# Two-layer decoder trunk on one core: expert stages in 64-slot units, two side by side in TensorE's output, with plain float32 products and 2-MB weight transfers

## The chip, the cores and the metric

One Trainium2 chip, one core. The metric is the device time of one execution in microseconds; the kernel before takes 2580.95 us in the median of three runs.

## The reference, cut to what matters

Two layers of a decoder over 1040 tokens (16 meta tokens and 1024), each a mixer followed by a channel mixer. The mixers (convolution and sparse attention; a gated recurrence) are not touched. The channel mixer is a routed mixture of 32 gated MLPs, and each token goes to 2 of them:

```python
def grouped_expert_ffn(xf, eid, w_gate, w_up, w_down):
    ...
    def run(args):
        xblk, e = args
        return (jax.nn.silu(xblk @ w_gate[e]) * (xblk @ w_up[e])) @ w_down[e]
    ...
def hierarchical_moe(h, wg, bg, we, be, w_gate, w_up, w_down):
    ...
    g_p, g_idx = lax.top_k(g_prob, 1)
    ...
    e_top, e_idx = lax.top_k(e_logits, TOP_K_INNER)
    gate = g_p * jax.nn.softmax(e_top, axis=-1)
    expert = (g_idx * EXPERTS_PER_GROUP + e_idx).reshape(-1)
    y_pairs = grouped_expert_ffn(xf, expert, w_gate, w_up, w_down).reshape(n_tok, TOP_K_INNER, d)
    y = jnp.einsum('nkd,nk->nd', y_pairs, gate.astype(y_pairs.dtype))
```

The width is 1024, the inner width of an expert 512, all in float32. An expert has three matrices of 2 MB (6.29 million bytes together). Layer 0 routes 2080 token-expert pairs, layer 1 (where only the 1024 tokens are kept) 2048.

## The kernel before, in words

The program is a list of stages; each stage writes out what every engine does, in order, with semaphores between them. The stage that changes is `experts` (L1878), called once for each layer. The layer-0 call runs from about 757 to 1424 us of the profiled span, the layer-1 call from about 1892 to 2544 us.

A stage first sorts the pairs by expert: `route` on VectorE turns counts into blocks of 128 slots, an expert having at least one block, and small matrix products (`slots`, L2401) put each pair's number into its slot. The result is a list in SBUF: the number of blocks, each block's expert, and whether it is another expert than the block before (`meta_i`). Engines read it into registers.

Then it works block by block, in a loop whose order is written out by hand:

- SyncE (`load`, `reload`, L1953 to L1972) fetches the expert's weights in six chunks of 1 MB (two each for gate, up and down) into `raw`, with a condition that skips a block of the same expert. A chunk may be overwritten once VectorE has split it (`lo_done`).
- GpSimd gathers 128 rows of h into `x` (L2006), and later adds 128 weighted rows of output to the sums in HBM with one accumulating scatter (`scatter`, L2010), waited for before `y` is free again. Slots that are not used carry an index out of bounds and move nothing.
- TensorE turns x (8 transposes, L2312) and hidden (4 transposes, L2323) and makes the products. Each float32 product is made from three float32r products (`mm3`, L90): high by high, high by low, low by high. Its order in a turn is gate for the next block (with the transposes of hidden in its middle), up for the next block, transposes of x for the one after, down for this block.
- ScalarE and VectorE split every weight chunk into a high and a low float32r part (L2066 and L2218), and x and hidden too; ScalarE makes silu (L2075) and takes y out of PSUM (L2084), VectorE multiplies silu by up (L2231).

```python
def mm3(pe, out, stat, mov, start, stop):
    pe.matmul(out, stat[0], mov[0], start=start, stop=False)
    pe.matmul(out, stat[0], mov[1], start=False, stop=False)
    return pe.matmul(out, stat[1], mov[0], start=False, stop=stop)
```

`stay_warm` (L97) makes plain float32 products of 256 columns that nothing reads, six or seven of them at a stage's start. Behind the layer-0 stage `combine` reads the sums back (L1875); in layer 1 the last two blocks stay on the chip and are added in `last_norm` (class `Rest`).

Of the kernel before, what the change touches and what calls it, by code (L numbers as in the profile page):

```python
# [43 lines left out]
MAXB = -(-(2 * T + NE * (P - 1)) // P)  # L44
# [23 lines left out]
C_ROW = C_IB + MAXB  # L68
# [1407 lines left out]
class Picks:  # L1476


    def __init__(self, c):
# [4 lines left out]
        self.is_l, self.is_h = (c.sb("pick_" + n, [P, 2, NB, P], BF16, side=RIGHT) for n in ("isl", "ish"))  # L1484
# [39 lines left out]
    def place(self, dve, link, const, work, ranks, B, first, read, nth, made):  # L1524
# [8 lines left out]
        link(dve.tensor_scalar(at_i[:, :, B], at_i[:, :, B], P - 1, None, ALU.bitwise_and))  # L1533
        link(dve.tensor_copy(self.at_p[:, :, B], at_i[:, :, B]))
        link(dve.tensor_tensor(self.over[:, :, B], at[:, :, B], self.at_p[:, :, B], ALU.subtract))
        for j in range(2):
            for b in range(B.start, B.stop):
                col = 2 * (first * NB + b) + j
                for dst, at_c in ((self.is_l, C_LOW), (self.is_h, C_PAIR)):
                    ins = dve.tensor_scalar(dst[:, j, b, :], const[:, C_I128:C_I128 + P], self.at_p[:, j, b:b + 1],  # L1540
                                            const[:, at_c + col:at_c + col + 1], ALU.is_equal, ALU.mult)
# [275 lines left out]
SUM_CHUNKS, GAIN_CHUNK = (2, 3, 4, 5, 0), 1  # L1817


class Rest:  # L1820


    def __init__(self, c, name, bank, sets):
        self.up = c.sb(name + "_wu", [P, 4, EXPERT_CHUNK], F32R)
        self.bank = bank
        self.acc = [bank[:, 0:2, :], bank[:, 4:6, :]][0:sets]

    def w_hi(self, i):
        return self.up[:, i - 2, :]

    def w_lo(self, i):
        return self.up[:, i, :]

    def y_hi(self, e):
        return self.up[:, 0, e * D:(e + 1) * D]

    def y_lo(self, e):
        return self.up[:, 2, e * D:(e + 1) * D]

    def place(self, e):  # L1840
        return self.up[:, 1 + 2 * e, 0:T]
# [10 lines left out]
class Sums:  # L1852
# [8 lines left out]
    def rows(self, n):  # L1861
        return self.raw[0:toks(self.blocks[n]), SUM_CHUNKS[n // 2], (n % 2) * D:(n % 2) * D + D]

    def gain(self, j):
        return self.raw[:, GAIN_CHUNK, j * D:(j + 1) * D]
# [12 lines left out]
def experts(nc, name, const, picks, h_d, sum_d, wg_d, wu_d, wd_d, first, raw, sums, rest=None):  # L1878


    CH, NCH = EXPERT_CHUNK, EXPERT_CHUNKS
    nb = NB - first
    B = slice(first, NB)
    n_tok = T if first == 0 else SEQ
    with Ctx(nc) as c:
        n_own = NCH if rest is None else NCH - 2
        own_hi, own_lo = c.sb(name + "whi", [P, n_own, CH], F32R), c.sb(name + "wlo", [P, n_own, CH], F32R)

        def chunk(i, own, kept):
            if rest is None:  # L1890
                return own[:, i, :]
            return kept(i) if i in (2, 3) else own[:, i if i < 2 else i - 2, :]

        w_hi = [chunk(i, own_hi, rest and rest.w_hi) for i in range(NCH)]
        w_lo = [chunk(i, own_lo, rest and rest.w_lo) for i in range(NCH)]
        x = c.sb(name + "x", [P, D])
        x_hi, x_lo = c.sb(name + "xh", [P, KC, P], F32R), c.sb(name + "xl", [P, KC, P], F32R)
        sg, hid = c.sb(name + "sg", [P, FE]), c.sb(name + "hid", [P, FE])
        h_hi, h_lo = c.sb(name + "hh", [P, FE // P, P], F32R), c.sb(name + "hl", [P, FE // P, P], F32R)
        y = c.sb(name + "y", [P, D])  # L1900
        ix, sx = c.sb(name + "ix", [P, 1], I32), c.sb(name + "sx", [P, 1], I32)
# [8 lines left out]
        cnt_i = c.sb(name + "_ci", [P, NE], I32)  # L1910
        start_of, at_r, at_b = (c.sb(name + n, [P, 2, NB]) for n in ("_so", "_ar", "_ab"))
        at_i = c.sb(name + "_ai", [P, 2, NB], I32)
        in_b, is_pf = c.sb(name + "_inb", [P, 2, NB, MAXB], BF16), c.sb(name + "_ispf", [P, 2, NB, P])
        wide_done = c.sem(name + "_wide")
        gates, is_g, by_slot = t3("_gates", 2), c.sb(name + "_isg", [P, 2, NB, MAXB]), c.sb(name + "_bys", [P, MAXB])
        pair_i, tok_i = c.sb(name + "_pair", [P, MAXB], I32), c.sb(name + "_tok", [P, MAXB], I32)
        of_blk, row = c.sb(name + "_ofb", [P, 1]), c.sb(name + "_row", [1, 2 * MAXB + 1])
        meta_i = c.sb(name + "_meta", [1, 2 * MAXB + 1], I32)
        N_AT, E_AT, R_AT = 0, 1, 1 + MAXB
# [5 lines left out]
        hi_done = [c.sem(name + f"_hi{i}") for i in range(NCH)]  # L1925
        lo_done = [c.sem(name + f"_lo{i}") for i in range(NCH)]
        chain, act_sem, count_mm, rank_mm, rank_read, placed, hot_b, slots_mm, blk_done, blk_mm, listed, indexed, hot_g, by_slot_mm, by_slot_done = (
            c.sem(name + n) for n in ("_c", "_a", "_cm", "_m", "_rr", "_pld", "_hb", "_sm", "_bd", "_bm", "_ls", "_in", "_hg", "_bym", "_byd"))
        primed, x_half, x_half_hi = (c.sem(name + n) for n in ("_primed", "_xhf", "_xhh"))
        x_zero, ix_done, sx_done, ix_taken, sx_taken, x_in, x_tr, x_hi_done, x_lo_done, g_mm, u_mm, sg_done, hid_done, h_tr, h_hi_done, h_lo_done = (  # L1930
            c.sem(name + n) for n in ("_xz", "_ix", "_sx", "_ixt", "_sxt", "_x_in", "_x_tr", "_x_hi", "_x_lo", "_g_mm", "_u_mm", "_sg", "_hid",
                                      "_h_tr", "_h_hi", "_h_lo"))
        y_mm, y_taken, y_stored, y_free = (c.sem(name + n) for n in ("_y_mm", "_y_taken", "_y_stored", "_y_free"))
# [4 lines left out]
        FIRST_LOADS = (0, 1, 2)  # L1938

        block = c.block()  # L1940

        def bc(t, w):
            return t[:, B, :].broadcast_to([P, nb, w])
# [4 lines left out]
        def blocks_but_two(eng):  # L1948
            eng.wait_ge(listed, 1)
            return eng.snap(eng.value_load(meta_i[0:1, N_AT:N_AT + 1], min_val=NE - 2, max_val=MAXB - 2))  # L1950
# [1198 lines left out]
```

## Time and profile before

| | |
|---|---|
| runs, us | 2576.66, 2580.95, 2582.27 (median 2580.95) |
| profiled execution: its span, us (the page gives no other time of it) | 2577.0 |
| TensorE matmuls busy | 2426.1 us, 94% |
| VectorE busy | 2025.5 us, 79% |
| ScalarE busy | 1683.3 us, 65% |
| GpSimd busy | 653.5 us, 25% |
| bytes moved by DMA | 565.81 MB, mean 220 GB/s |
| expert stage of layer 0 | 757.2 to 1424.1 us |
| expert stage of layer 1 | 1891.5 to 2544.0 us |

Busy time is the union of an engine's instructions. Matmul records overlap, since each has its pipeline's length in it, so the pace of TensorE is read from one start to the next. A DMA share of 1 means that the core's 16 DMA engines had packets all the time.

### The profile page before, as it was taken

How to read it: one execution, taken by the hardware profiler on the slowest of the kernel's cores; microseconds unless marked ns; L12 is line 12 of the kernel's file. 1: busy time of each engine (PE TensorE's matmuls, PEld its weight loads, DVE VectorE, ACT ScalarE, POOL GpSimd, SP SyncE). 2: the span in 40 equal slices, each digit the busy share in tenths (PEclk: the TensorE clock that was granted, in tenths of full speed). 3: DMA queues.
4: the chain of work that ended last, by engine and by line, in shares of the span. 5: the costliest groups of instructions: out<-in, count | busy, mean ns of one | idle time of the engine just before them, and what ended most of it. 6: DMA issues, size and time to landing. Idle time of an engine off the chain costs nothing. (4 is left out here: it accounts for less than half of the span.)

```text
span 2577.0 us, 37706 instructions
## 1 busy us (share of the span) xinstructions
PE 2426.1 (94%) x12715; PEld 2077.8 (81%) x12715; DVE 2025.5 (79%) x2589; ACT 1683.3 (65%) x1814; POOL 653.5 (25%) x480
## 2 busy tenths in 40 slices
PE   9989998987979999999999599999979999999997
PEld 8979978885867888888888499997867888888885
DVE  4788876777889989999898544547779998998887
ACT  3369836666227788887887466663147888877775
POOL 0105814343002222222221412121013222223232
PEclk9999999997989999999999699999989999999999
DMA  5502354324349699988998411114259699999995
GB/s 181 134 13 87 83 99 128 105 67 136 101 148 405 228 346 375 366 322 316 320 376 290 173 58 36 39 34 159 94 204 356 234 353 369 376 370 363 376 373 191
DMA packets 121902, 565.81 MB, mean 220 GB/s; under 512 B 24119, under 2 KB 32567, under 8 KB 72528
## 3 DMA queue, kind: packets, MB, share of 16 engines
q1 hardware_dynamic: 96688, 513.25, 55.1%
q0 software_dynamic: 25120, 51.36, 7.2%
q8 instruction: 54, 0.88, 0.1%
q14 instruction: 40, 0.33, 0.0%
HBM read 575.32 MB, written 73.28 MB: 252 GB/s over the span
## 5 line engine op out<-in xcount | busy, mean ns | idle before, releaser
L2218 DVE TENSOR_TENSOR e0wlo<-e0raw,e0whi 128x2048 fp32r<-128x2048 f32 x214 | 487.1, 2290 | 59.8 <-ACT e0whi L2066 59.8
L2066 ACT ACTIVATE e0whi<-e0raw 128x2048 fp32r<-128x2048 f32 x214 | 409.9, 1915 | 90.3 <-PE e0banks L94 78.2
L2218 DVE TENSOR_TENSOR e1wlo<-e1raw,e1whi 128x2048 fp32r<-128x2048 f32 x138 | 313.2, 2286 | 43.4 <-ACT e1whi L2066 43.2
L2066 ACT ACTIVATE e1whi<-e1raw 128x2048 fp32r<-128x2048 f32 x138 | 263.9, 1913 | 40.0 <-PE e1banks L94 33.5
L92 PE MATMUL e0banks<-e0whi,e0xh 128*128 128x512 f32 x576 | 231.1, 401 | 2.9 <-DVE e0xl L2223 2.7
L94 PE MATMUL e0banks<-e0whi,e0xl 128*128 128x512 f32 x576 | 226.1, 392 | 0.0
L93 PE MATMUL e0banks<-e0wlo,e0xh 128*128 128x512 f32 x576 | 225.6, 392 | 0.0
L2218 DVE TENSOR_TENSOR e_wu<-e1raw,e_wu 128x2048 fp32r<-128x2048 f32 x70 | 160.2, 2290 | 17.8 <-ACT e_wu L2066 17.7
L92 PE MATMUL odd_banks<-h2T_hi,odd_w_hi 128*128 128x348 f32 x480 | 171.6, 357 | 0.8 <-DVE h2T_lo L2539 0.5
L2066 ACT ACTIVATE e_wu<-e1raw 128x2048 fp32r<-128x2048 f32 x70 | 134.2, 1918 | 50.4 <-PE e1banks L94 30.7
L93 PE MATMUL odd_banks<-h2T_lo,odd_w_hi 128*128 128x348 f32 x480 | 155.1, 323 | 0.0
L94 PE MATMUL odd_banks<-h2T_hi,odd_w_lo 128*128 128x348 f32 x480 | 155.1, 323 | 0.0
L92 PEld LDWEIGHTS e0banks<-e0whi,e0xh 128*128 128x128 f32 x576 | 108.6, 189 | 32.7 <-issue 11.3
L94 PEld LDWEIGHTS e0banks<-e0whi,e0xl 128*128 128x128 f32 x576 | 108.5, 188 | 23.2
L93 PEld LDWEIGHTS e0banks<-e0wlo,e0xh 128*128 128x128 f32 x576 | 108.8, 189 | 20.9
L92 PE MATMUL e1banks<-e1whi,e1xh 128*128 128x512 f32 x280 | 115.6, 413 | 6.4 <-DVE e1xl L2223 6.4
L2472 DVE TENSOR_TENSOR odd_w_lo<-odd_w_raw,odd_w_hi 128x1024 fp32r<-128x1024 f32 x18 | 22.3, 1239 | 119.4 <-ACT odd_w_hi L2468 119.4
L92 PE MATMUL e0banks<-e0whi,e0hh 128*128 128x512 f32 x280 | 112.1, 400 | 0.0
L94 PE MATMUL e1banks<-e1whi,e1xl 128*128 128x512 f32 x280 | 110.6, 395 | 0.0
L93 PE MATMUL e1banks<-e1wlo,e1xh 128*128 128x512 f32 x280 | 110.3, 394 | 0.0
L92 PE MATMUL e1banks<-e_wu,e1xh 128*128 128x512 f32 x280 | 109.1, 390 | 0.2 <-DVE e_wu L2218 0.2
L94 PE MATMUL e1banks<-e_wu,e1xl 128*128 128x512 f32 x280 | 109.2, 390 | 0.0
(526 smaller groups left out, 6898.2 us busy)
## 6 DMA issues: line engine op xcount, KB each, us to landing
e0raw<-in_moe_w_gate SPq DMA_DIRECT2D x72, 1024.0 KB
e0raw<-in_moe_w_up SPq DMA_DIRECT2D x72, 1024.0 KB
e0raw<-in_moe_w_down SPq DMA_DIRECT2D x72, 1024.0 KB
e1raw<-in_moe_w_gate SPq DMA_DIRECT2D x70, 1024.0 KB
e1raw<-in_moe_w_up SPq DMA_DIRECT2D x70, 1024.0 KB
e1raw<-in_moe_w_down SPq DMA_DIRECT2D x70, 1024.0 KB
qki_w_raw<-in_w_even SPq DMA_DIRECT2D x22, 512.0 KB, 5.8
pre<-in_conv_band SPq DMA_DIRECT2D x32, 320.0 KB, 3.0
```

What stands on the lines that cost most here:

```text
L92: pe.matmul(out, stat[0], mov[0], start=start, stop=False)
L93: pe.matmul(out, stat[0], mov[1], start=False, stop=False)
L94: return pe.matmul(out, stat[1], mov[0], start=False, stop=stop)
L2066: act.activation(w_hi[i], raw[:, i, :], ACT.Copy).then_inc(hi_done[i], 1)
L2218: dve.tensor_tensor(w_lo[i], raw[:, i, :], w_hi[i].bitcast(F32), ALU.subtract).then_inc(lo_done[i], 1)
L2472: eng.tensor_tensor(self.w_lo[:, n % 2, :], self.raw[:, n % 2, :], self.w_hi[:, n % 2, :].bitcast(F32), ALU.subtract).then_inc(self.lo_don ...
```

## The change

- Slots are counted in units of 64 (`UNIT`), and the units of a layer are laid in two halves: column g has unit g in partitions 0 to 63 and unit g + half in 64 to 127. The list now has an entry for each unit, and the number of columns.
- The products are plain float32: no high and low parts, no splits on ScalarE and VectorE. Each product of 128 stationary columns becomes two of 64, `both`: one per half, with that half's own expert's weights, into partitions 0 to 63 and 64 to 127 of the same bank.
- Six whole matrices are held (three for each half), raw only, each fetched as one 2-MB transfer once the products of the one before it have been made (`used`). A transfer is skipped where the half's expert stays.
- x and hidden are copied from PSUM once; ScalarE takes the first half of x, VectorE the second.
- The scatter is made in two parts, one per half, each waited for before the next.

```diff
-MAXB = -(-(2 * T + NE * (P - 1)) // P)
+UNIT = P // 2
+MAXU = (2 * T + NE * (UNIT - 1)) // UNIT
+MAXC = -(-MAXU // 2)
...
-            def reload(chunks, g):
-                e = sp.value_load(meta_i[0:1, bass.ds(g + E_AT, 1)], min_val=0, max_val=NE - 1)
-                new = sp.value_load(meta_i[0:1, bass.ds(g + R_AT, 1)], min_val=0, max_val=1)
-                for i in chunks:
-                    sp.wait_ge(lo_done[i], g)
-                    load(i, e, new)
+            def load(w, s, e, new=None, into=None):
+                into = 3 * s + (w if into is None else into)
+                src = (wg_d, wu_d, wd_d)[w][bass.ds(e, 1), :, :].rearrange("a (p c) n -> (a p) c n", p=P)
+                dst = whole[into].rearrange("p (c n) -> p c n", c=(8, 8, 4)[w])
...
+            def reload(matrices, g):
+                e = [expert_of(u) for u in (g, g + half)]
+                new = [sp.value_load(meta_i[0:1, bass.ds(u + R_AT, 1)], min_val=0, max_val=1) for u in (g, g + half)]
+                for w in matrices:
+                    sp.wait_ge(used[2 * w + 1], g)
+                    for s in range(2):
+                        load(w, s, e[s], new[s])
+            for w in range(3):
+                load(w, 0, 0)
+            m = columns_but_two(sp)
+            half = sp.snap(sp.value_load(meta_i[0:1, H_AT:H_AT + 1], min_val=NE // 2, max_val=MAXC))
+            e = expert_of(half)
+            for w in range(3):
+                load(w, 1, e)
+            reload((0, 1), 1)
+            reload((0, 1), 2)
+            reload((2,), 1)
...
-                pool.indirect_dma_start(sum_d, bass.IndirectOffsetOnAxis(sx[:, 0:1].bitcast(U32), 0), y[:], None,
-                                        bounds_check=n_tok - 1, oob_is_err=False, compute_op=ALU.add).then_inc(y_stored, 16)
-                pool.wait_ge(y_stored, g * 16 + 16)
-                pool.sem_inc(y_free, 1)
+                for s in range(2):
+                    pool.indirect_dma_start(sum_d, bass.IndirectOffsetOnAxis(sx[:, s:s + 1].bitcast(U32), 0), rows[:], None,
+                                            bounds_check=n_tok - 1, oob_is_err=False, compute_op=ALU.add).then_inc(y_stored[s], 16)
+                    pool.wait_ge(y_stored[s], stored)
+                    pool.sem_inc((y_half, y_free)[s], 1)
...
             def turn(g):
-                split_h(g)
-                for i in WG:
-                    split_w(i, g + 2)
+                take_h(g)
                 silu(g + 1)
-                for i in WU:
-                    split_w(i, g + 2)
-                split_x(g + 2)
-                split_w(4, g + 1)
+                take_x(g + 2)
                 take_y(g)
-                split_w(5, g + 1)
...
-                link(dve.tensor_scalar(cnt_i[:], xt_ps[:, 1, 0:NE], float(P - 1), None, ALU.add))
-                link(dve.tensor_scalar(cnt_i[:], cnt_i[:], 7, None, ALU.arith_shift_right))
+                link(dve.tensor_scalar(cnt_i[:], xt_ps[:, 1, 0:NE], float(UNIT - 1), None, ALU.add))
+                link(dve.tensor_scalar(cnt_i[:], cnt_i[:], 6, None, ALU.arith_shift_right))
                 link(dve.tensor_scalar(nblk[:], cnt_i[:], 1.0, None, ALU.max))
                 link(dve.tensor_tensor_scan(pend[:], one32[:], nblk[:], 0.0, ALU.mult, ALU.add))
+                link(dve.tensor_scalar(half_i[:], pend[:, NE - 1:NE], 1.0, None, ALU.add))
+                link(dve.tensor_scalar(half_i[:], half_i[:], 1, None, ALU.arith_shift_right))
+                link(dve.tensor_scalar(half_f[:], half_i[:], float(UNIT), None, ALU.mult))
...
+            def both(out, stat, chunk, a, start, stop):
+
+                for s in range(2):
+                    last = pe.matmul(out[HALF[s], :], stat[:, HALF[s]], raw[NCH * s + chunk][:, a], start=start, stop=stop)
+                return last
...
                 for k in range(4 * (i % 2), 4 * (i % 2) + 4):
-                    a = slice((k % 4) * FE, (k % 4 + 1) * FE)
-                    last = mm3(pe, ps[:], (x_hi[:, k, :], x_lo[:, k, :]), (w_hi[i][:, a], w_lo[i][:, a]),
-                               k == 0, k == KC - 1)
+                    last = both(ps, xt[:, k, :], i, slice((k % 4) * FE, (k % 4 + 1) * FE), k == 0, k == KC - 1)
                 last.then_inc(used[i], 1)
```

How the order of instructions moves. First TensorE, in the loop of the layer-0 stage, from the end of up to the start of down (`e0x` is x, `xh`/`xl` and `hh`/`hl` the parts of turned x and hidden, `xt` and `ht` the same turned and whole, `e0raw` and `e0own` homes of raw weights). Before:

```order
L92 MATMUL e0banks<-e0whi,e0xh 128x512
L93 MATMUL e0banks<-e0wlo,e0xh 128x512
L94 MATMUL e0banks<-e0whi,e0xl 128x512
L2308 ISA
L2312 MATMUL e0banks<-const,e0x 128x128 x8
L92 MATMUL e0banks<-e0whi,e0hh 128x512
L93 MATMUL e0banks<-e0wlo,e0hh 128x512
L94 MATMUL e0banks<-e0whi,e0hl 128x512
```

and now, from the loop's start:

```order
L2224 MATMUL e0banks<-e0own,e0xt 64x512 x8
L2249 MATMUL e0banks<-const,e0hid 128x128 x4
L2224 MATMUL e0banks<-e0own,e0xt 64x512 x8
L2224 MATMUL e0banks<-e0raw,e0xt 64x512 x16
L2233 ISA
L2238 MATMUL e0banks<-const,e0x 128x128 x8
L2230 ISA
L2224 MATMUL e0banks<-e0raw,e0ht 64x512
L2224 MATMUL e0banks<-e0own,e0ht 64x512
```

The order of gate, transposes, up and down stays. What was three products of 128x512 is two of 64x512, and the full-width transposes stand between the half-width products twice in a turn.

Second GpSimd, the same loop, from the gather on. Before:

```order
L2037 COPY e0ix<-e_tok 128x1
L2038 REGISTER_ALU
L2006 DMA e0x<-h,e0ix 128x1024
L2012 ISA
L2012 COPY e0sx<-e_tok 128x1
L2015 DMA sum<-e0y,e0sx 1040x1024
L2017 ISA
```

and now:

```order
L2024 COPY e0ix<-e_tok 128x1
L2025 REGISTER_ALU
L1992 DMA e0x<-h,e0ix 128x1024
L1998 ISA
L1998 COPY e0sx<-e_tokh 128x2
L2002 DMA sum<-e0y,e0sx 1040x1024
L2004 ISA
L2002 DMA sum<-e0y,e0sx 1040x1024
```

The second scatter, behind the first one's wait, stands ahead of the next gather. Third SyncE, the loads of the loop, now:

```order
L1947 DMA e0own<-in_moe_w_gate 128x4096
L1947 ISA
L1947 DMA e0own<-in_moe_w_gate 128x4096
L1947 DMA e0raw<-in_moe_w_up 128x4096 x2
L1950 ISA
L1950 TENSOR_LOAD e_meta
```

There were six of 128x2048 to a turn; there are six of 128x4096, with eight reads of the list instead of four.

## Rows read from the trace of the kernel before

**Rows 1.** The page: its span and part 1, engines' busy time.
```profile
span 2577.0 us, 37706 instructions
...
PE 2426.1 (94%) x12715; PEld 2077.8 (81%) x12715; DVE 2025.5 (79%) x2589; ACT 1683.3 (65%) x1814; POOL 653.5 (25%) x480
```

**Rows 2.** Windows (first line: columns): the expert stages of both layers.
```profile
core 0: us, PE busy (x) PEld busy (x) DVE busy (x) ACT busy (x) POOL busy (x), PEclk, DMA share, GB/s
757.20:1424.10 666.90, 656.93 (x3118) 541.24 (x3118) 594.13 (x373) 522.28 (x366) 152.86 (x143) 0.99 0.89 330
1891.50:2544.00 652.50, 638.48 (x3026) 525.68 (x3027) 582.74 (x371) 506.82 (x357) 168.00 (x136) 0.99 0.93 343
```

**Rows 3.** Timeline (start and length in us, engine, line, operation): TensorE in layer 0.
```profile
999.62 0.39 PE L93 MATMUL e0banks<-e0wlo,e0xh 128*128 128x512 f32 x1
...
999.85 0.19 PEld L92 LDWEIGHTS e0banks<-e0whi,e0xh 128*128 128x128 f32 x1
...
1001.21 0.39 PE L94 MATMUL e0banks<-e0whi,e0xl 128*128 128x512 f32 x1
```

**Rows 4.** SyncE: timeline from 856 us, its waits in layer 0.
```profile
856.41 2.51 SPq L1963 DMA_DIRECT2D e0raw<-in_moe_w_gate  x2
...
892.41 0.34 SPq L1963 DMA_DIRECT2D e0raw<-in_moe_w_gate  x1
...
SPq L1963 <- DVE e0wlo L2218: 392.7, 193, 4.7
```

**Rows 5.** The page, part 6: gate weights, two transfers to a block.
```profile
e0raw<-in_moe_w_gate SPq DMA_DIRECT2D x72, 1024.0 KB
...
e1raw<-in_moe_w_gate SPq DMA_DIRECT2D x70, 1024.0 KB
```

**Rows 6.** Windows: four stretches of layer 0's stage.
```profile
757.00:770.00 13.00, 6.16 (x53) 5.00 (x54) 11.36 (x47) 6.49 (x6) 3.18 (x4) 0.50 0.80 295
...
790.00:820.00 30.00, 27.51 (x121) 22.48 (x122) 28.80 (x18) 23.16 (x16) 11.21 (x4) 0.94 1.02 419
840.00:900.00 60.00, 60.00 (x287) 49.65 (x286) 54.48 (x32) 48.05 (x34) 13.90 (x14) 1.00 0.63 217
940.00:1100.00 160.00, 160.00 (x755) 132.01 (x754) 145.42 (x81) 128.80 (x91) 37.33 (x36) 1.00 0.99 371
```

**Rows 7.** Groups by line: layer 0's weight splits.
```profile
L2218 DVE TENSOR_TENSOR e0wlo<-e0raw,e0whi 128x2048 fp32r<-128x2048 f32 x214 | 487.1, 2290 | 59.8 <-ACT e0whi L2066 59.8
L2066 ACT ACTIVATE e0whi<-e0raw 128x2048 fp32r<-128x2048 f32 x214 | 409.9, 1915 | 90.3 <-PE e0banks L94 78.2 <-DMA e0raw<-in_moe_w_gate 5.8 <-DMA e0raw<-in_moe_w_up 5.0
```

**Rows 8.** Timeline: plain float32 products, six warm, seven at a stage's start.
```profile
185.32 2.75 PE L100 MATMUL ix_banks<-const 128*128 128x256 f32 x12
...
766.16 5.17 PE L100 MATMUL e0banks<-const 128*128 128x256 f32 x14
```

**Rows 9.** Timeline of TensorE: the first transposes, and those of a turn.
```profile
771.55 1.16 PE L2312 MATMUL e0banks<-const,e0x 128*128 128x128 f32 x8 [0.21 <-DMA e0x<-h,e_tok]
...
1002.12 1.05 PE L2312 MATMUL e0banks<-const,e0x 128*128 128x128 f32 x8
...
1415.27 0.60 PE L2323 MATMUL e0banks<-const,e0hid 128*128 128x128 f32 x4
```

**Rows 10.** GpSimd: one turn in the timeline, and the landing of y's transfers.
```profile
975.67 1.60 POOL L2015 DMA_INDIRECT sum<-e0y,e0sx  x1 [0.89 <-POOL e0sx L2012]
987.65 1.61 POOL L2037 COPY e0ix<-e_tok 128x1 int32 x1 [10.38 <-DMA sum<-e0y,e0sx]
...
993.49 1.61 POOL L2015 DMA_INDIRECT sum<-e0y,e0sx  x1 [0.89 <-POOL e0sx L2012]
...
DMA to landing us min/median/max: 2.0/8.9/14.5
```

**Rows 11.** Timeline: the end of layer 0's stage.
```profile
1428.29 1.54 POOL L2052 DMA_INDIRECT sum<-e0x,e0ix  x1 [5.66 <-issue]
1432.95 0.80 SPq L1875 DMA_DIRECT2D e0raw<-sum  x2
```

More of the change, by code:

```diff
@@ L1875, in load_rows, with experts @@
             sp.dma_start(self.rows(n), self.sum_d[at:at + toks(b), :]).then_inc(self.loaded[n], 16)
-def experts(nc, name, const, picks, h_d, sum_d, wg_d, wu_d, wd_d, first, raw, sums, rest=None):
-    CH, NCH = EXPERT_CHUNK, EXPERT_CHUNKS
+def experts(nc, name, const, picks, h_d, sum_d, wg_d, wu_d, wd_d, first, kept_raw, sums, rest=None):
+    NCH = EXPERT_CHUNKS
     nb = NB - first
@@ L1884, in experts @@
     n_tok = T if first == 0 else SEQ
+    HALF = (slice(0, UNIT), slice(UNIT, P))
     with Ctx(nc) as c:
[L1886 to L1899, printed above, removed]
+        own_chunks = [i for i in range(2 * NCH) if i not in KEPT_CHUNKS]
+        own_raw = c.sb(name + "own", [P, len(own_chunks), EXPERT_CHUNK])
+        whole = [home[:, at:at + 2, :].rearrange("p a n -> p (a n)")
+                 for home, at in ((own_raw, 0), (kept_raw, 0), (kept_raw, 4), (own_raw, 2), (kept_raw, 2), (own_raw, 4))]
+        raw = [kept_raw[:, KEPT_CHUNKS.index(i), :] if i in KEPT_CHUNKS else own_raw[:, own_chunks.index(i), :] for i in range(2 * NCH)]
+        x, xt = c.sb(name + "x", [P, D]), c.sb(name + "xt", [P, KC, P])
+        sg, hid, ht = c.sb(name + "sg", [P, FE]), c.sb(name + "hid", [P, FE]), c.sb(name + "ht", [P, FE // P, P])
         y = c.sb(name + "y", [P, D])
-        ix, sx = c.sb(name + "ix", [P, 1], I32), c.sb(name + "sx", [P, 1], I32)
+        ix, sx = c.sb(name + "ix", [P, 1], I32), c.sb(name + "sx", [P, 2], I32)
         tok_f, tok_n, gate2 = c.sb(name + "_tf", [P, 2]), c.sb(name + "_tn", [P, 2, NB - 1]), c.sb(name + "_g2", [P, 2])
@@ L1974, in _ @@
[L1974 to L1988 removed]
+                    sp.dma_start(dst, src, cond=new).then_inc(landed[into], 16)
@@ L1989, in _ @@
+            e = [expert_of(u) for u in (m + 1, m + 1 + half)]
+            sp.wait_ge(used[1], m + 2)
+            for s in range(2):
+                load(2, s, e[s], into=0)
             if rest is None:
-                sp.wait_ge(lo_done[1], m + 3)
+                sp.wait_ge(used[5], m + 1)
                 sums.load_gains(sp)
-                sp.wait_ge(y_stored, m * 16 + 32)
+                sp.wait_ge(y_stored[1], m * 16 + 32)
                 sums.load_rows(sp, BEFORE_CHANGE)
             else:
-                sp.wait_ge(y_stored, m * 16)
@@ L2401, in slots @@
             def slots(j, b, start, stop):
-                pe.matmul(ht_ps[:, 0:MAXB], is_l[:, j, b, :], in_b[:, j, b, :], start=start, stop=False)
-                return pe.matmul(ht_ps[:, 0:MAXB], is_h[:, j, b, :], in_b[:, j, b, :], start=False, stop=stop)
+                for table, opens, ends in ((is_l, start, False), (is_h, False, stop)):
+                    for s in range(2):
+                        last = pe.matmul(ht_ps[HALF[s], 0:MAXC], table[:, j, b, :], in_b[:, j, b, s, :], start=opens, stop=ends)
+                return last
             for j in range(2):
@@ L2428, in _ @@
                 for b in range(first, NB):
-                    last = pe.matmul(y_ps[:, 0, 0:MAXB], is_pf[:, j, b, :], is_g[:, j, b, :], start=j == 0 and b == first,
-                                     stop=j == 1 and b == NB - 1)
+                    for s in range(2):
+                        last = pe.matmul(y_ps[HALF[s], 0, 0:MAXC], is_pf[:, j, b, :], is_g[:, j, b, s, :], start=j == 0 and b == first,
+                                         stop=j == 1 and b == NB - 1)
             last.then_inc(by_slot_mm, 1)
```

324 lines of the change are left out of this document (110 added, 214 removed).

## The prediction, as it was put on record

> **What bounds the kernel now.** I read the busy times first, then each expert stage as a window, then a piece of its timeline. [rows 1] show TensorE as the busiest engine. The two expert stages take 666.9 and 652.5 us of the 2577.0 us span, and in both TensorE is busy 98% of the time at full granted clock, with DMA at 0.89 and 0.93 [rows 2]. Inside a stage one float32r product of 512 columns starts every 0.227 us ([rows 3]: from 999.62 to 1001.21 are seven steps), and a block has 72 of them, which is 16.3 us. With the transposes that gives the period of some 18 us that SyncE's issues show (856.41 to 892.41 are two blocks) [rows 4]. 36 and 35 such blocks (72 and 70 gate transfers, two to a block) make up the stages [rows 5]. So TensorE sets the pace and the DMA engines are close behind: at 790 to 820 us, where a queue of work was waiting, they moved 419 GB/s at a share of 1.02; at 940 to 1100 us they were full at 371 GB/s, though no engine waited for them; where an expert has a second block they are at 0.63 [rows 6].
>
> **What is removed.** Per block, six splits on ScalarE and six on VectorE (1.92 and 2.29 us each, [rows 7]) go, with the splits of x and hidden. They are 410 and 487 us busy in layer 0, and none of them is worth anything by itself: TensorE's own gaps in these stages are 10 of 667 us [rows 2]. I cost them at nothing; their cover is TensorE.
>
> **Units instead of blocks.** The blocks of 128 slots become units of 64, two units to a column. Counting the tokens that the reference's own routing gives each expert for its inputs, I get 36 and 35 blocks, as the trace has, and 49 and 50 units, so 25 columns in either layer.
>
> **TensorE per column.** A plain float32 product leaves two records: seven products of 256 columns are 14 records, six are 12 [rows 8]. Warm, 12 such records take 2.75 us, the last being 0.38 long, so one starts every 0.215 us for 256 columns, and a 512-column product takes 2 x 0.431 = 0.862 us. A column has 24 pairs of products (8 gate, 8 up, 8 down), one for each half of the output. What a pair costs is shown by no row: no product of the kernel before runs in part of the columns beside another. It lies between 0.862 us (the halves run together) and 1.724 us (one after the other). I take 0.862: the two share neither output rows nor stationary columns, and moving operands come in at 256 columns per 0.215 us, half the rate at which float32r products already draw them (512 in 0.227 us), so two streams ask for no more than what is drawn today. The Trainium skill (TensorE: Matmul & The Clock Gate, Part 3) says that output tiles in different column groups run concurrently, with 2.38 times the rate measured for three of them. Read as an efficiency of 0.79 for two, an estimate by that page would be 1.09 us a pair; that is a rival below. The same page says, against this change, that a weight load overlaps a running product only when the row group differs. [rows 3] speak against that: loads of 0.19 us lie inside products that use all 128 rows, every 0.227 us. So I cost the four loads of a pair at nothing; if they lay open they would add at most 4 x 0.19 = 0.76 us to it, which is near rival 2.
>
> So a column is 24 x 0.862 = 20.7 us, plus transposes of x (1.05) and of hidden (0.60) [rows 9]. The array now changes between full products and half products four times; no row prices that. I take 0.2 us each, about one float32r product's start to start [rows 3], between the ends 0 and 0.4 (two of them). Sum 23.1 us; 25 of them are 578 us. The first transposes start 14.4 us into the stage (771.55 less 757.2) [rows 9], and I add 1 us for three more links on VectorE and the doubled slot products. That gives 594 us with no wait for weights.
>
> **Weights.** Each layer still loads 32 experts of 6.29 MB. Of the 419 GB/s, gathers and scatters take 2080 rows x 4 KB x 2 = 17 MB in 667 us, 26 GB/s, so weights get about 390. A 2-MB transfer takes 5.4 us, a column with two new experts 32.3 us, one with one 16.1. The numbers of new experts in the columns behind the first are, in layer 0, 0 2 0 2 1 1 1 0 2 1 0 1 1 1 2 2 1 2 2 2 2 1 2 1, in layer 1, 0 1 2 2 1 2 0 2 1 2 1 1 1 1 0 1 1 2 1 1 2 2 2 1. There is one buffer per matrix and half now, raw only: the gate weights of the next column can start when this column's gate products end (before, when VectorE had split a chunk). I walked the columns with that rule, in the order gate, up, down. TensorE waits 51 us in layer 0 and 38 us in layer 1. Bounds of the wait are nothing and 10 x (32.3 - 23.1) = 92 us in layer 0 (ten columns with two new experts; nine in layer 1). In it are some 6 us at the start: the second half's gate weights are only asked for once the list is known, behind the three matrices of the first half. Columns 15 to 24 of layer 0 carry most of the rest. Stages: 645 and 632 us. SyncE reads twice as many list values per column and issues six transfers as before; it stood waiting 393 of the stage's 667 us [rows 4], so nothing for that.
>
> A TensorE that waits may lose its clock. At the start of layer 0's stage, after such a stretch, 14 records that would take 3.2 us warm took 5.2 us [rows 8], and the granted clock was 0.50 for those 13 us [rows 6]: a fall costs about 2 us. In a weight-bound column each matrix leaves 10.8 - 6.9 = 3.9 us of waiting, so the loss would lie inside the wait. Cost nothing; without that cover, three falls in each of some 19 columns would be 114 us.
>
> **GpSimd.** The loop now has two accumulating scatters, each waited for, and they hold y. Transfers of y land after 8.9 us in the median, 14.5 at most, and the one shown took 12.0 [rows 10]. From its landing to the next scatter are 5.8 us of copies and issues, 1.0 of it a longer copy. An iteration is then 4.8 + 2 x 8.9 = 22.6 us, under a column's 23.1 and with 16 us of slack until the next down products need y read. I cost it at nothing inside. At the end of layer 0 a second scatter stands in the open: from issue at 1428.29 to the load of the sums at 1432.95 is 4.7 us [rows 11], so 5 us. Layer 1's last scatter is hidden. The longer routing adds 3 for both layers, an estimate: some eight more instructions of 0.2 us each.
>
> **Sum.** (645 - 667) + (632 - 652) + 8 = -34 us: 2577 to 2543. The median of the runs is 4 us above this span, so 2547 us.
>
> **Rivals.**
> 1. *Halves only partly overlap.* At 1.09 us a pair a column takes 28.6 us and hides nearly all transfers: stages of 740 and 738 us, +159 + 8, so about 2748 us: slower. The change decides against itself from 0.92 us a pair on. For it: no row shows two halves at once. Against it: the draw on the operands above.
> 2. *No overlap.* 1.724 us a pair: 1118 us a stage, about 3510 us. The change's own side-by-side would not happen.
> 3. *DMA gives weights only 345 to 365 GB/s*, which is what 371 GB/s at a full share at 940 to 1100 us leaves. At 345: 690 and 677 us, +56, about 2637 us; at 365: 667 and 654 us, about 2591. For it: share 0.99 there. Against: TensorE asked for no more there (6.29 MB per 17.8 us is 353 GB/s), and 419 was reached before.
> 4. *Scatters in a row set the pace.* If each of the two took 11.6 us, between the median and the longest, an iteration would be 28 us and a stage 15.5 + 25 x 28 = 716 us, so about 2700 us. The median speaks against it, and that each half has under 64 rows.
> 5. *Quicker weights.* At 418 GB/s and no cost for the changes of shape, 613 and 602 us: about 2484 us.
>
> **How the numbers follow.** Forecast, with 390 to 400 GB/s and 0.86 to 0.90 us: 0.53; rival 5 or near: 0.10; rival 3: 0.11; rival 1: 0.12; rival 2: 0.08; rival 4: 0.06. The forecast's own range is 2515 to 2575. The range reaches from 2480 to 2710: it leaves out rivals 1 and 2 alone. About 0.2% is what a measurement of this kernel tells from no change (5 us). Faster 0.62 (forecast, rival 5, little of 3), the same 0.04, slower 0.34.
>
> **What would show it.** The half products should have starts in pairs: four records per 0.86 us. One record per 0.43 us is rival 2. VectorE and ScalarE should fall below half their busy time in the stages. TensorE's waits should be put down to weight transfers, bunched in columns 15 to 24 of layer 0, with DMA share 1 there. If waits name x or y instead, the scatters have taken over. The granted clock should stay at 1.0 outside the weight-bound columns; if waits of 3 to 5 us bring it to half, that is a term I left at nothing. The prediction is wrong if a pair takes more than 0.92 us.

## The result: 2619 us, slower, where I forecast 2547

| | before | changed |
|---|---|---|
| median of the runs, us | 2579.9 (4 runs) | 2619.06 (4 runs, 2612.79 to 2622.95) |
| profiled span, us | 2577.0 | 2621.2 |
| expert stage of layer 0, us | 666.9 | 677.6 |
| expert stage of layer 1, us | 652.5 | 672.4 |
| the rest of the span, us | 1257.6 | 1271.2 |

The ratio is 1.0153, with a 95% interval of 1.0133 to 1.0173. I forecast two shorter stages, 645 and 632 us. The page of the changed kernel (its busy times, and q0, the queue of GpSimd's transfers, with its packets, MB and share of the DMA engines' time):

```profile
span 2621.2 us, 34528 instructions
PE 2332.9 (89%) x12287; PEld 1459.4 (56%) x12287; DVE 968.0 (37%) x2068; ACT 801.0 (31%) x1302; POOL 556.4 (21%) x444
q0 software_dynamic: 25984, 51.26, 7.3%
```

VectorE and ScalarE gave up more than half their work, as the change says (before, [rows 1]). TensorE, which sets the pace, is busy less, and the program is longer. The windows of the two stages, the answer to [rows 2], and two stretches of layer 0 (columns as there):

```profile
757.90:1435.50 677.60, 601.77 (x2866) 223.78 (x2866) 58.35 (x108) 73.69 (x105) 110.51 (x121) 0.95 0.85 328
1912.10:2584.50 672.40, 598.26 (x2851) 222.13 (x2851) 62.19 (x115) 73.39 (x106) 109.37 (x119) 0.95 0.86 332
...
1000.00:1100.00 100.00, 95.26 (x448) 34.35 (x446) 6.92 (x8) 12.35 (x17) 21.15 (x23) 0.98 0.77 267
1200.00:1300.00 100.00, 81.60 (x364) 29.65 (x362) 5.19 (x6) 10.69 (x15) 17.21 (x20) 0.91 0.98 395
```

TensorE is busy 601.8 of 677.6 us where it was 656.9 of 666.9, and the granted clock is 0.95 instead of 0.99. DMA share is below 1 on average: neither TensorE nor the DMA engines are full.

**The products themselves do what was forecast.** A column in which nothing waits, in TensorE's timeline:

```profile
1057.00 0.66 PE L2249 MATMUL e0banks<-const,e0hid 128*128 128x128 f32 x4
1057.59 3.65 PE L2224 MATMUL e0banks<-e0own,e0xt 128*64 128x512 f32 x16
1061.07 7.04 PE L2224 MATMUL e0banks<-e0raw,e0xt 128*64 128x512 f32 x32
1068.04 1.16 PE L2238 MATMUL e0banks<-const,e0x 128*128 128x128 f32 x8
...
1074.76 0.59 PE L2224 MATMUL e0banks<-e0raw,e0ht 128*64 128x512 f32 x1
1074.77 0.59 PE L2224 MATMUL e0banks<-e0own,e0ht 128*64 128x512 f32 x1
1075.19 0.59 PE L2224 MATMUL e0banks<-e0raw,e0ht 128*64 128x512 f32 x1
1075.20 0.59 PE L2224 MATMUL e0banks<-e0own,e0ht 128*64 128x512 f32 x1
...
1079.58 0.66 PE L2249 MATMUL e0banks<-const,e0hid 128*128 128x128 f32 x4
```

Records of the two halves start together, a new pair of records each 0.43 us: four records in 0.86 us. The whole column takes 1079.58 - 1057.00 = 22.58 us. The Trainium skill (TensorE: Matmul & The Clock Gate, Part 3) lets output tiles of different column groups run concurrently, with less than the full gain for three; here two take no longer than one.

**What TensorE waits for** (engine, line, releaser: total us, times, longest):

```profile
PE e1banks L2238 <- DMA e1x<-h,e1ix: 24.5, 9, 7.9
PE e0banks L2238 <- DMA e0x<-h,e0ix: 21.0, 7, 10.0
PE e1banks L2224 <- DMA e1raw<-in_moe_w_up: 18.1, 8, 3.2
PE e0banks L2224 <- DMA e0raw<-in_moe_w_up: 16.2, 8, 2.8
PE e0banks L2224 <- DMA e0own<-in_moe_w_gate: 14.6, 7, 3.7
PE e1banks L2224 <- DMA e1own<-in_moe_w_gate: 11.4, 7, 3.1
PE e0banks L2224 <- DMA e0own<-in_moe_w_down: 8.8, 4, 2.7
PE e0banks L2238 <- DMA e0x<-h,e_tok: 7.8, 1, 7.8
PE e1banks L2238 <- DMA e1x<-h,e_tok: 7.7, 1, 7.7
```

Weights are there as forecast, in many short waits. Beside them stand gathers of x, 45 us in the two loops, which I had said would be a sign that the scatters have taken over. Why a gather is late is in GpSimd's timeline:

```profile
1181.99 1.58 POOL L2002 DMA_INDIRECT sum<-e0y,e0sx  x1 [0.85 <-POOL e0sx L1998]
1198.83 1.55 POOL L2002 DMA_INDIRECT sum<-e0y,e0sx  x1 [15.26 <-DMA sum<-e0y,e0sx]
1211.37 0.19 POOL L2024 COPY e0ix<-e_tok 128x1 int32 x1 [10.99 <-DMA sum<-e0y,e0sx]
1212.46 1.07 POOL L1992 DMA_INDIRECT e0x<-h,e0ix  x1 [0.90 <-ACT e0y L2054]
```

Two landings in a row, 16.8 and 12.5 us from issue to the next instruction, stand ahead of the gather. What follows on TensorE:

```profile
1209.78 3.60 PE L2224 MATMUL e0banks<-e0raw,e0xt 128*64 128x512 f32 x16
1223.34 1.97 PE L2238 MATMUL e0banks<-const,e0x 128*128 128x128 f32 x8 [9.95 <-DMA e0x<-h,e0ix]
1225.24 1.12 PE L2224 MATMUL e0banks<-e0raw,e0ht 128*64 128x512 f32 x1
...
1228.70 0.64 PE L2224 MATMUL e0banks<-e0raw,e0ht 128*64 128x512 f32 x1
```

After the wait of 9.95 us the transposes take 1.97 us instead of 1.16, and four pairs of records 3.46 us (1225.24 to 1228.70) instead of 1.71: the clock is at its lower level, for 5.4 us, and the wait costs 2.6 us beyond itself.

To get a stage's account, I took every start of a TensorE record behind the first product and subtracted from its distance to the one before what the undisturbed column has. Excess before a transposition of x counts as a wait for x, any other of over 0.45 us or at a change of operation as a wait for weights (the waits above agree), and excess between like records as half clock. Start is from the first transfer to the first product.

| layer 0 / layer 1, us | start | 25 columns | x | weights | half clock | stage |
|---|---|---|---|---|---|---|
| forecast | 15.5 | 578 | 0 | 51 / 38 | 0 | 645 / 632 |
| measured (columns: 25 x 22.58) | 26.0 / 26.1 | 564.5 | 21.5 / 25.2 | 43.1 / 38.1 | 22.8 / 19.8 | 677.6 / 672.4 |

The terms add up to 677.9 and 673.7 us, since every record is held against one reference column. The column headed half clock is not all of one kind. Held against the granted clock in the trace, TensorE is at its lower level for 52 us of layer 0 in all, and the records that start there hold some 20 of the 22.8 us; the rest is small excess at full clock.

The start differs by what stands on the queue. SyncE and the gather, changed kernel:

```profile
757.87 0.33 SPq L1945 DMA_DIRECT2D e0own<-in_moe_w_gate  x1
758.25 0.43 SPq L1945 DMA_DIRECT2D e0raw<-in_moe_w_up  x1
758.73 0.43 SPq L1945 DMA_DIRECT2D e0raw<-in_moe_w_down  x1
771.60 0.35 SPq L1945 DMA_DIRECT2D e0own<-in_moe_w_gate  x1
```

The kernel before listed 3 MB there and then waited for x; now it is 6.29 MB, and the first gather, issued at 769.1, lands only at 780.7. The second half's gate weights are asked for at 771.60, and the first product comes at 783.9.

### The profile page after: what moved, and what is told of

The parts are those of the page before. It is cut to its first block and busy times, and to the rows that moved or that the text cites. A ratio compares the mean times of both kernels' runs of the same rounds, so it can differ in the third digit from the quotient of the medians.

```text
span 2621.2 us, 34528 instructions
## 1 busy us (share of the span) xinstructions
PE 2332.9 (89%) x12287; PEld 1459.4 (56%) x12287; DVE 968.0 (37%) x2068; ACT 801.0 (31%) x1302; POOL 556.4 (21%) x444
## 3 DMA queue, kind: packets, MB, share of 16 engines
q0 software_dynamic: 25984, 51.26, 7.3%
## 5 line engine op out<-in xcount | busy, mean ns | idle before, releaser
L2224 PE MATMUL e0banks<-e0own,e0xt 128*64 128x512 f32 x832 | 197.0, 618 | 16.0 <-DMA e0own<-in_moe_w_gate 14.6
L2224 PE MATMUL e1banks<-e1own,e1xt 128*64 128x512 f32 x832 | 192.4, 605 | 13.8 <-DMA e1own<-in_moe_w_gate 11.4
L2224 PE MATMUL e0banks<-e0raw,e0xt 128*64 128x512 f32 x800 | 183.0, 611 | 16.2 <-DMA e0raw<-in_moe_w_up 16.2
L2224 PE MATMUL e1banks<-e1raw,e1xt 128*64 128x512 f32 x800 | 179.9, 602 | 18.1 <-DMA e1raw<-in_moe_w_up 18.1
L2224 PE MATMUL e0banks<-e0raw,e0ht 128*64 128x512 f32 x384 | 175.8, 611 | 7.5 <-DMA e0own<-in_moe_w_down 7.4
L2224 PE MATMUL e1banks<-e1raw,e1ht 128*64 128x512 f32 x384 | 179.1, 621 | 2.6 <-DMA e1own<-in_moe_w_down 2.6
L2224 PE MATMUL e1banks<-e1own,e1ht 128*64 128x512 f32 x384 | 179.2, 621 | 0.0
L2224 PE MATMUL e0banks<-e0own,e0ht 128*64 128x512 f32 x384 | 175.9, 612 | 0.0
L2002 POOL DMA_INDIRECT sum<-e0y,e0sx x48 | 75.1, 1566 | 278.9 <-DMA sum<-e0y,e0sx 257.6
L2002 POOL DMA_INDIRECT sum<-e1y,e1sx x46 | 72.0, 1564 | 282.2 <-DMA sum<-e1y,e1sx 262.5
```

The lines of the kernel that those rows point to most:

```text
L2002: pool.indirect_dma_start(sum_d, bass.IndirectOffsetOnAxis(sx[:, s:s + 1].bitcast(U32), 0), rows[:], None, bounds_check=n_tok - 1, oob_is_ ...
L2224: last = pe.matmul(out[HALF[s], :], stat[:, HALF[s]], raw[NCH * s + chunk][:, a], start=start, stop=stop)
```

## The experiments

Each was timed beside the kernel before on its chip (2575.6 to 2578.9 us there); times are medians, each with its ratio to the kernel before and the 95% interval. The changed kernel is 2619 us, 1.0153 (1.0133 to 1.0173).

### One scatter and gather at a time

**The order at the start.**

```diff
-            for w in range(3):
+            for w in range(2):
                 load(w, 0, 0)
...
-            for w in range(3):
+            for w in range(2):
                 load(w, 1, e)
+            load(2, 0, 0)
+            load(2, 1, e)
```

> Undoes one part: at a stage's start only gate and up of the first half are listed before the list of experts is read; then gate and up of the second half, then both down matrices. The changed kernel takes 2619 us. Theory A (the start is late because 6.29 MB stand on the queue ahead of the first gather of x, landing 11.6 us after its issue against some 4.3 before, and ahead of the second half's gate weights): the first gather lands in 4 to 6 us, the first product comes 7 to 9 us earlier in each layer, about 2603 us. Rival B (the longer routing and the doubled list are what is late): the first gather is issued no earlier and the gain is at most 2 us a layer, 2615 to 2619 us.

Measured: 2613.2 us, 1.0136 (1.0119 to 1.0152) of before. The first gather does land after 4.4 us, but the first product comes 22.9 us into the stage, only 3.1 us earlier: it now waits for the second half's gate weights, which land 9 us after their issue. A is half right: the queue made x late, and behind x stood a second thing that was nearly as late. In the profiled run, the slowest of the six (2625.1 us), the waits for x in layer 0 are 44.7 us instead of 21.5, so that its stages are no shorter together (683.7 and 671.1 us). The medians differ by 6 us, about what two starts give, but the two intervals overlap: the earlier start is shown by the trace, the gain in time is not clear of noise.

**The gather ahead of the second landing.**

```diff
+            next_x(0)
+            scatter(0)
+            with pool.Fori(1, before_m) as g:
+                next_x(g)
+                stored(pool.snap(g * 16 + 16))
+                scatter(g)
```

(`next_x` is the copy of the index and the gather, `stored` the wait for the second scatter, taken out of `scatter`.)

> GpSimd issues the gather of x for the column after next behind the issue of the second scatter, and waits for that scatter's landing only afterwards; nothing else differs from the changed kernel (2619 us). Theory A (two scatters and a gather in one chain of waits set the pace where weights don't): TensorE's waits for x in front of the transposes, 21.5 and 25.2 us, nearly vanish, some of it comes back as waits for weights, about 2590 us (range 2575 to 2600). Rival C (the weight transfers set the pace, and a wait for x only stands where a wait for weights would have come): within 5 us of 2619.

Measured: 2592.5 us, 1.0064 (1.0047 to 1.0081). Its waits:

```profile
PE e0banks L2239 <- DMA e0raw<-in_moe_w_up: 27.6, 10, 4.8
PE e1banks L2239 <- DMA e1raw<-in_moe_w_up: 24.5, 9, 4.1
PE e1banks L2239 <- DMA e1own<-in_moe_w_gate: 17.5, 8, 4.2
PE e0banks L2239 <- DMA e0own<-in_moe_w_gate: 15.9, 7, 3.9
```

No wait for x is left in the loops, and weights rise from 43.1 and 38.1 to 54.1 and 49.9 us. So x cost some 26 us net (23 by the ratios), as theory A had it; C falls.

**One scatter.** The loop over the halves in `scatter` has one turn instead of two.

> The second half's scatter is left out, so half of the experts' outputs are not added; one scatter per column remains. Theory A: GpSimd's turn falls from some 25 to some 15 us, no wait for x is left but the first one, about 2575 us (2565 to 2595), near the kernel with the gather first or a little below. Rival C (weights alone): within 5 us of 2619.

Measured: 2586.1 us, 1.0030 (1.0014 to 1.0046). No wait for x, weights 56.9 and 49.0 us. With half of layer 0's outputs missing, layer 1 routes other tokens: its transfers are those of 100 matrices of 2 MB instead of 97. So only layer 0 compares, and its stage is 670.9 us here and 668.5 with the gather first. Taking a whole scatter out gives no more than moving the gather: once the gather is out of the chain, the second scatter costs next to nothing inside the loop. At the end of layer 0 TensorE's longest wait for the sums is 20.5 us here and 31.5 us with the gather first, which is more than the 6 us between the two.

**No weight transfers in the loop.**

```diff
-                                       row[0:1, E_AT:E_AT + MAXU - 1], ALU.not_equal))
+                                       row[0:1, E_AT:E_AT + MAXU - 1], ALU.is_lt))
```

> The weight transfers of the loop are skipped (each half keeps the weights it began with), so all experts but the first of each half are computed with wrong weights; the transfers at the start and for the last down product remain. Theory A: a column is 22.6 us of TensorE with no wait, scatters land in under half their 10 us, the granted clock stays at 1.0 behind the start; stages of 26 + 25 x 22.6 = 591 us each instead of 678 and 672, so about 2452 us (2445 to 2465). Rival D (half-array products lose the clock by themselves, waits or not): clock 0.95 as now and some 25 us more, about 2480 us. Rival E (scatters are slow by themselves, not from the weight traffic): landings stay at 10 us, GpSimd's turn of 25 us sets the pace, about 2520 us.

Measured: 2435.5 us, 0.9449 (0.9433 to 0.9465). Its layer 1 has other tokens to route, since layer 0's output is another, and one column less, so only layer 0 is compared: its stage takes 595.3 us where I expected 591, hardly a wait is left, the half-clock column of the account falls from 22.8 to 6.3 us, and both chains move freely. Of the 6.3 us some 2 are at the lower clock, all in the first 4 us behind the first product; the rest is small excess at full clock.

```profile
785.00:1350.00 565.00, 563.88 (x2754) 203.74 (x2752) 43.08 (x53) 70.95 (x98) 106.79 (x116) 1.00 0.19 43
```

The time from issue to landing, as the page's part 6 has it:

```profile
sum<-e0y,e0sx POOLq DMA_INDIRECT x48, 6.0
```

The granted clock is 1.00 without waits, so the half-array products don't lose it by themselves; that leaves the waits. A scatter lands after 6.0 us in the median instead of 11.0 (below): nearly half its landing goes with the weight traffic. D and E both fall.

### The size and the order of the transfers

**1-MB transfers.** Each matrix is fetched in two parts, each with a landing semaphore of its own.

```diff
                 for w in matrices:
-                    sp.wait_ge(used[2 * w + 1], g)
-                    for s in range(2):
-                        load(w, s, e[s], new[s])
+                    for part in range(2):
+                        sp.wait_ge(used[2 * w + part], g)
+                        for s in range(2):
+                            load(w, s, e[s], new[s], parts=(part,))
```

> Undoes the 2-MB transfers alone: each matrix is fetched as two of 1 MB, each asked for when its own half of the products has been made, with a landing semaphore of its own. The changed kernel takes 2619 us. Theory A (part of TensorE's 42 and 36 us of waits for weights comes from asking late, since a whole matrix has to be used up first): transfers start up to 3.5 us earlier and the first half can be used before the second has landed, about 2600 us. Rival F (the transfers are short of bandwidth where TensorE waits, or GpSimd's chain fills the time): within 5 us of 2619. Rival G (smaller transfers are slower by themselves): 2630 us or more.

Measured: 2548.2 us, 0.9879 (0.9864 to 0.9894): faster than before. The gain of 71 us is over three times what A said. The edit does three things at once: smaller transfers, each half asked for earlier, and products that begin when half a matrix has landed. The same stretch of layer 0's stage in the changed kernel, and then with 1 MB:

```profile
785.00:1350.00 565.00, 512.56 (x2411) 187.85 (x2409) 38.65 (x48) 59.46 (x85) 92.80 (x101) 0.96 0.84 322
```

```profile
785.00:1350.00 565.00, 530.22 (x2526) 193.40 (x2522) 40.26 (x50) 65.28 (x91) 100.34 (x110) 0.98 0.91 342
```

DMA engines are at 0.91 of their time instead of 0.84. Waits for x fall to 0.5 and 3.9 us, weights to 41.9 and 26.9 although nothing of x hides them any more, half clock to 18.1 and 13.4, the start to 23.5 and 24.2.

**1 MB, but asked for whole.** `sp.wait_ge(used[2 * w + 1], g)` for both parts, and products that wait for both.

> Transfers of 1 MB as in the kernel that gave 2548 us, but both of a matrix are asked for only when the whole matrix has been used, and products begin only when both have landed, as with 2 MB. It tells the size of a packet (8192 bytes instead of 16384, in the trace 309 and 611 ns each) apart from the finer asking. Theory P (packets: a scatter's 9 packets on each DMA engine each wait behind a weight packet, so shorter ones shorten the landing, from 10.1 to 8.8 us, and take the waits for x away): scatters land in 8.8 us, waits for x nearly gone, about 2585 us. Theory Q (the finer asking alone gave the 71 us, since weights then never bunch up): landing as with 2 MB and about 2615 us. If both are worth what the parts suggest, 2580 to 2595 us with the rest up to 2548 due to the finer asking.

Measured: 2606.7 us, 1.0120 (1.0091 to 1.0150). The smaller transfers by themselves gave 12 us by the medians and 9 by the ratios, whose intervals overlap (1.0133 to 1.0173 with 2 MB), so some 10 of the 71 us at most are theirs, hardly clear of noise. Some 60 come from asking and using in halves: Q is nearly right. Asking and using changed together, and no run tells them apart. Landings, changed kernel:

```profile
sum<-e0y,e0sx POOLq DMA_INDIRECT x48, 11.0
sum<-e1y,e1sx POOLq DMA_INDIRECT x46, 11.1
```

and here:

```profile
sum<-e0y,e0sx POOLq DMA_INDIRECT x48, 9.0
sum<-e1y,e1sx POOLq DMA_INDIRECT x46, 9.6
```

P's shorter landings are there, by 1.5 to 2 us, and no wait for x is left. But weights take their place, 63.0 and 52.2 us, until they are asked for in halves.

**The halves apart.** Gate and up make the four products of a chunk for the first half, and then for the second.

```diff
-                for k in range(4 * (i % 2), 4 * (i % 2) + 4):
-                    last = both(ps, xt[:, k, :], i, slice((k % 4) * FE, (k % 4 + 1) * FE), k == 0, k == KC - 1)
+                for s in range(2):
+                    for k in range(4 * (i % 2), 4 * (i % 2) + 4):
+                        last = one(s, ps, xt[:, k, :], i, slice((k % 4) * FE, (k % 4 + 1) * FE), k == 0, k == KC - 1)
```

> The same products as the changed kernel, but gate and up make the four products of a chunk for the first half and then the four for the second, instead of in turn; down stays in turn. If halves run together only where neighbouring products go to different halves, 16 pairs of a column cost 1.71 us instead of 0.86: 13.8 us more per column less what the seams overlap, weights are hidden, and the time is about 3100 us (3050 to 3150). If products of the two halves run together whatever their order, 2619 us.

Measured in a single run: 2694.2 us, neither. A gate chunk of 16 records, ahead of the transposes of hidden, in the changed kernel:

```profile
1076.05 3.60 PE L2224 MATMUL e0banks<-e0own,e0xt 128*64 128x512 f32 x16
1079.58 0.66 PE L2249 MATMUL e0banks<-const,e0hid 128*128 128x128 f32 x4
```

and here:

```profile
1069.87 5.37 PE L2222 MATMUL e0banks<-e0own,e0xt 128*64 128x512 f32 x16
1075.17 0.66 PE L2251 MATMUL e0banks<-const,e0hid 128*128 128x128 f32 x4
```

5.3 us instead of 3.5, where one after the other would be 6.9. The single starts are four records alone, 0.428 us apart (1069.87 to 1071.16), then four pairs (first at 1071.59 and 1071.60), then four alone. By this count the fifth product of the program started beside the third. Where gate ends and up begins, the records name the matrices (`e0own` gate, `e0raw` up):

```profile
1075.76 4.13 PE L2222 MATMUL e0banks<-e0own,e0xt 128*64 128x512 f32 x13
1079.31 0.64 PE L2222 MATMUL e0banks<-e0raw,e0xt 128*64 128x512 f32 x1
1079.73 0.59 PE L2222 MATMUL e0banks<-e0own,e0xt 128*64 128x512 f32 x1
```

Up's first product starts at 1079.31, while three of the sixteen records of gate, which stand ahead of it in the program, have not started. A column takes 26.3 us (down to down, 1069.87 to 1096.21): 3.8 us more than in turn, not 13.8. 25 columns of that are 94 us a stage; waits and half clock give back 87.4 - 29.7 = 58 of them in layer 0, and its stage is 38.5 us longer.

**Scatters of 64 rows.** The second half's indices are copied to partitions 0 to 63, and each scatter hands over `rows[HALF[s], :]` with `sx[0:UNIT, s:s + 1]`.

> Each scatter hands over only its own 64 rows of y and 64 indices instead of 128 with 64 out of bounds. Leaving out 48 scatters took 6912 packets with it, 144 each, so a scatter's packets should fall to about 72. Theory A with a landing that goes by packets: landing 10.1 us falls to 7, GpSimd's turn falls below TensorE's column, waits for x go, about 2595 us. Rival H (the landing goes by the weight packets that stand ahead on the same DMA engines): landing stays at 10 us and the time within 5 us of 2619.

Measured: 2588.5 us, 1.0044 (1.0028 to 1.0059). Landings are 8.7 and 8.6 us in the median, waits for x gone. A holds, though landings fall less than it said. GpSimd's queue has 19840 packets instead of 25984: 64 fewer in each of 96 scatters, all of 8 bytes, with the packets of rows (4096 bytes) unchanged in number. An index out of bounds moves no row, but has a packet of its own. That this packet waits its turn is argued from the landings.

**Transfers of 512 KB.** Each 1-MB transfer as two.

> As the kernel with 1-MB transfers (2548 us), but each as two of 512 KB, so packets of 4096 bytes; asking and waiting as there. Theory P: with packets of some 159 ns instead of 309 a scatter's landing falls by up to 9 x 0.15 = 1.3 us to 7.5 us; GpSimd no longer sets the pace there, so the time falls little, 2540 to 2548 us. Rival G (small packets carry less: 4096 bytes in 159 ns is 3% less than 8192 in 309): 2555 to 2565 us, weight waits longer.

Measured: 2570.4 us, 0.9983 (0.9970 to 0.9997). Landings fall to 7.9 and 8.3 us, near what P says, but weights cost 46.7 and 40.2 us instead of 41.9 and 26.9. The time is on G's side and 5 us beyond its range. From 1200 to 1300 us, with 1 MB and then with 512 KB:

```profile
1200.00:1300.00 100.00, 82.68 (x350) 30.14 (x348) 5.13 (x6) 9.31 (x13) 15.59 (x18) 0.91 1.02 412
```

```profile
1200.00:1300.00 100.00, 79.31 (x334) 29.11 (x332) 5.17 (x6) 9.82 (x13) 15.50 (x17) 0.92 1.03 403
```

The rate falls by 2%, as G says. Something else changed too: twice as many transfers are issued. What SyncE waited for between 785 and 1350 us, with 1 MB and then with 512 KB:

```profile
SPq L1952 <- PE e0banks L2231: 314.3, 119, 9.7
SPq L1954 <- PE e0banks L2233: 107.0, 66, 9.0
```

In that stretch its issues of transfers take 222 us instead of 78, the longest 4.2 us. So transfers may also have been asked for late because SyncE was behind. No run tells this from G.

### All that helped, together

> Gather of x ahead of the second scatter's landing (worth 26 us alone), the second half's gate and up weights ahead of both down matrices at the start (6 us alone), 1-MB transfers and scatters of 64 rows together. If the gains add: 2619 less 26, 6 and 15 to 20 for the transfers, about 2570 us (2555 to 2590), just below the kernel before at 2578. If weights are short of bandwidth in the heavy columns the transfers' size gives nothing and it is 2587.

Measured: 2525.1 us, 0.9796 (0.9782 to 0.9809), 54 us faster than before and 94 faster than the change. Stages take 636.1 and 617.1 us; the start is 20.1 and 20.3 us, x costs nothing, weights 40.7 and 26.6, half clock 11.7 and 7.4. A scatter lands in 7.1 and 7.6 us.

> The combined kernel (2525 us) with 512-KB transfers. Theory P: 2520 to 2528 us. Rival G: 2530 to 2540 us.

Measured: 2549.9 us, 0.9895 (0.9879 to 0.9912): slower again, by 10 us more than G said. SyncE's issues grow here as well (80 to 221 us between 785 and 1350 us), so the same two causes stand.

## Why the prediction was wrong, point by point

In one sentence: two terms that I put at nothing, GpSimd's chain of landings and TensorE's clock behind its waits, cost 47 and 43 us over both layers, and the start, at 15.5 us a layer, measured 26.

- *A pair is 0.862 us, and loads and changes of shape cost little.* Right. The pair is 0.856 us, the column 22.58 us where I had 23.1. Rivals 1 and 2 did not happen. This was the step I thought most about, and it was 13 us a stage on the safe side.
- *GpSimd: "I cost it at nothing inside".* The step that failed first. I took the landing from the kernel before, 8.9 us, into an iteration of 22.6. The median over both layers is 11 us with 2-MB transfers, so an iteration, estimated as in the prediction, is 4.8 + 22 = 26.8 us against a column of 22.58, and in layer 1 even the old landings were 10.1. It is rival 4 nearly as written (28 us), which I gave 0.06. It did not reach its 716 us a stage, since columns that wait for weights hide part of it: 21.5 and 25.2 us of waits, 26 us net by the gather's own run.
- *"Cost nothing" for the clock.* Failed too: 22.8 and 19.8 us, of which some 20 in layer 0 are at the lower clock (17 in layer 1). I had argued that the loss lies inside a wait for weights. It lies behind it, as in the wait of 9.95 us above: the records after it run at half rate. It is over a third of the 114 us that I named for the case without cover.
- *The start, 15.5 us.* 26.0. I took the first gather's landing from a queue with 3 MB on it, though the diff puts 6.29 MB there. I priced the instructions that were added and not the queue they go past.
- *Weights: 51 and 38 us.* The size was right (43.1 and 38.1, and 54.1 and 49.9 with nothing else hiding them), the reason for it was half right. I treated it as set by 390 GB/s and one buffer. The two runs with 1-MB transfers show that a good part comes from the rule that a whole matrix must be used before the next is asked for, and must have landed before it is used. I walked that rule and never asked what the other one would give. It is no reason why the forecast missed, but handling a matrix as a whole is what makes the change slower than the kernel before: in halves it is faster (0.9879).
- *The end of layer 0, 5 us.* From the stage's end to the load of the sums it is 1455.2 - 1435.5 = 19.7 us, against 8.9 before: 10.8. Two columns, so four landings, stand in a row there, where before the last two scatters were one each.

Together, in layer 0: 645 - 13 + 10.5 - 8 + 21.5 + 22.8 = 679 us, and 677.6 were measured. The DMA rate of rival 3 did not come: 395 GB/s at a share of 0.98.

The Trainium skill (DMA: Bandwidth & Descriptors, Queues, rings and completion order) says that a DMA engine goes round its queues a packet at a time. The trace fits this: a scatter of 128 indices, which the run with one scatter prices at 144 packets (6912 for 48), is 9 per engine; a weight packet of 16384 bytes takes 611 ns in the median and one of 8192 bytes 309. Nine of each are 5.5 and 2.8 us, an estimate for what a landing loses to the traffic; 11.0 - 6.0 = 5.0 and 9.0 - 6.0 = 3.0 were measured. That the packets take turns is argued from these numbers, and not shown by itself. The same page's rule (Bandwidth) to batch to 1 MiB or more speaks neither for 2 MB nor against it; here 512 KB lost 22 us, and 2 MB some 10 by its size and some 60 because a matrix was asked for and used whole.

The rest of the span is 13.6 us longer where I had 8; the end of layer 0 is most of it.

Left open: why the fastest kernel's layer 0 still has TensorE at the lower clock for 17 us (some 8 of its 11.7 us), once at its start and four times behind 1200 us, with no wait above 3.2 us; how much of layer 0's end could go; and what part of the 60 us is asking and what part is using in halves. No run here tried a second set of weight buffers.

## What to carry to other kernels

When a change makes transfers larger, the landing of every other transfer and the moment at which a buffer may be refilled change with it: price both, and try the old size with the new code before judging the new code. A chain of waits on an engine that is busy only 21% of the time is a rate like any other: add up its landings, as they will be under the new traffic, against the new period. A wait on TensorE can cost more than its length, here 2.6 us more for one of 10 us.

## What the runs showed of the hardware that I had not expected

- Products for different halves of the output ran together although others stood between their places in the program (the halves apart): up's first product started at 1079.31 us, ahead of three records of the gate products before it.
- An index that is out of bounds is not free: with 64 of them left out a scatter landed 2.3 us sooner (11.0 to 8.7), and 64 packets of 8 bytes went with them from each scatter.
- Whole matrices fetched as 2-MB transfers used the DMA engines less well than 1-MB ones in this kernel (0.84 against 0.91), and not because of their rate when they ran: asked for as wholes, 1-MB transfers moved 410 GB/s at a share of 1.01 from 1200 to 1300 us, and the kernel was still some 60 us slower than with the same ones asked for in halves.
